# A fused gather layer: tokens ordered by thirty-two on the partitions, weighted sums in eight tiles of 64 by 32, gates on ScalarE

## The reference

```python
def one_block(xb):                      # 128 tokens
    q = jnp.einsum('nd,dc->nc', xb, w_query).reshape(PEER_BLOCK, PEER_HEADS, 2, PEER_QUERY_DIM // 2)
    s = jnp.einsum('nhpc,hpkc->nhpk', q, subkeys).astype(jnp.float32)
    sv, si = lax.top_k(s, PEER_TOPK)
    ...
    top_s, pos = lax.top_k(cand_s, PEER_TOPK)
    experts = jnp.take_along_axis(cand_i, pos, axis=-1).reshape(PEER_BLOCK, PEER_HEADS * PEER_TOPK)
    gates = jax.nn.softmax(top_s, axis=-1).reshape(PEER_BLOCK, PEER_HEADS * PEER_TOPK)
    u = u_table[experts]
    hid = jax.nn.gelu(jnp.einsum('nkd,nd->nk', u, xb).astype(jnp.float32), approximate=False) * gates
    return jnp.einsum('nk,nkd->nd', hid.astype(xb.dtype), v_table[experts])
```

## Time and profile before

| | us |
|---|---|
| median of three runs | 1961.75 (1961.67 to 1966.66) |
| the profiled execution | 1955.42 |
| its span, first to last instruction | 1953.6 |
| PE, DVE, ACT, POOL busy | 1634.3, 1328.8, 656.3, 600.0 |

### The profile page before, as it was taken

One profiled execution on the slowest core, in us unless ns is written; L12 is line 12 of the kernel. 1 busy time (PEld: TensorE's weight loads), 2 busy tenths in 40 slices (PEclk: granted clock), 3 DMA queues, 4 the chain that ended last, 5 costly groups with the idle time before them and its releaser, 6 DMA issues.

```text
span 1953.6 us, 19684 instructions
## 1 busy us (share of the span) xinstructions
PE 1634.3 (84%) x6534; PEld 799.7 (41%) x6534; DVE 1328.8 (68%) x3466; ACT 656.3 (34%) x1224; POOL 600.0 (31%) x529
## 2 busy tenths in 40 slices
PE   7987897779889976888589999789986877877998
PEld 7555553235455443244145434333333322322453
DVE  4356877875788797875876577976665569744242
ACT  3222424242343254222231233521221246311472
POOL 1002333432333343334433333343323325422000
PEclk9997998889999998889899999899998988899999
DMA  7559999999999998999999999999999999999863
GB/s 223 179 169 416 417 417 419 408 417 418 386 413 354 355 416 326 380 419 415 422 413 418 418 414 374 362 400 418 419 417 350 418 419 401 421 418 412 326 235 109
DMA packets 128836, 729.03 MB, mean 373 GB/s; under 512 B 14688, under 2 KB 15856, under 8 KB 63200
## 3 DMA queue, kind: packets, MB, share of 16 engines
q0 software_dynamic: 74272, 537.82, 67.5%
q1 hardware_dynamic: 54464, 189.97, 25.5%
HBM read 725.63 MB, written 2.10 MB: 373 GB/s over the span
## 4 chain that ended last, share of the span: by engine, by line
PE 47%; DMA 23%; DVE 18%; ACT 5%; issue 5%; POOL 1%; POOLq 0%; DVEq 0%; SPq 0%; ACTq 0%
PE pa L919 26%; DMA uv_rows<-in_peer_uv,small 14%; PE py L919 13%; DMA wbuf<-in_wt 8%; PE pb L919 7%; DVE uv_rows L2046 6%; ACT area L1371 2%; ACT L1365 2%; POOL uv_rows L2291 1%; DVE tk L2056 1%; DVE area L2144 1%; DVE tk L2055 1%; DVE small L2033 1%; ACT small L1371 1%; DVE small L1951 0%
## 5 line engine op out<-in xcount | busy, mean ns | idle before, releaser
L2291 POOL DMA_INDIRECT uv_rows<-in_peer_uv,small x512 | 592.2, 1157 | 1182.3 <-PE py L919 967.2
L2046 DVE CUSTOM_DVE_ANT_0 uv_rows<-uv_rows,xrep 128x1024 f32<-128x1024 f32 x512 | 615.7, 1223 | 223.5 <-DMA uv_rows<-in_peer_uv,small 220.6
L919 PE MATMUL py<-uv_rows,tk 128*64 128x512 f32 x2048 | 560.8, 674 | 211.8 <-DVE tk L2056 208.1
L919 PE MATMUL pa<-wbuf,area 128*128 128x512 f32 (+2 forms) x784 | 342.0, 587 | 27.4 <-DMA wbuf<-in_wt 26.7
L1371 ACT ACTIVATE small<-small 128x2 f32<-128x2 f32 (+4 forms) x327 | 70.6, 217 | 849.9 <-DVE small L2046 816.2
L919 PEld LDWEIGHTS py<-uv_rows,tk 128*64 128x64 f32 x2048 | 135.7, 148 | 514.6 <-DVE tk L2056 278.3
L1365 ACT ACT_TABLE_LOAD x250 | 320.8, 1283 | 5.4 <-DVE small L2177 1.0
L919 PE MATMUL pa<-area,wbuf 128*128 128x256 f32 (+2 forms) x1280 | 233.7, 341 | 17.5 <-issue 12.0
L919 PEld LDWEIGHTS pa<-area,wbuf 128*128 128x128 f32 x1280 | 201.3, 199 | 70.6 <-issue 44.5
L919 PEld LDWEIGHTS pa<-wbuf,area 128*128 128x128 f32 (+1 forms) x784 | 134.2, 189 | 229.5 <-issue 176.5
L1371 ACT ACTIVATE area<-pa 128x512 f32<-128x512 f32 (+7 forms) x225 | 89.2, 413 | 267.3 <-PE pa L919 238.0
(11 more groups left out here) (253 smaller groups left out, 1178.0 us busy)
## 6 DMA issues: line engine op xcount, KB each, us to landing
wbuf<-in_wt SPq DMA_DIRECT2D x300, 512.0 KB
uv_rows<-in_wt SPq DMA_DIRECT2D x36, 512.0 KB, 6.6
uv_rows<-in_peer_uv,small POOLq DMA_INDIRECT x512
wbuf<-in_skT SPq DMA_DIRECT2D x11, 256.0 KB
h<-in_x SPq DMA_DIRECT2D x4, 512.0 KB
an<-in_x SPq DMA_DIRECT2D x3, 512.0 KB
out<-h SPq DMA_DIRECT2D x3, 512.0 KB, 8.3
area<-in_finw SPq DMA_DIRECT2D x2, 512.0 KB, 10.1
```

The costliest lines, as they stand in the source:

```text
L919: return nc.tensor.matmul(o, l, r, start=start, stop=stop, skip_group_check=True)
L2046: last = V.tensor_tensor_reduce(uv_rows[:, n % RING, 0:D], uv_rows[:, n % RING, 0:D], xrep[:, b % 2, n % TG, :], 1.0, 0.0, ALU.mult, ALU.a ...
L2291: nc.gpsimd.indirect_dma_start(uv_rows[:, n % RING, :], None, t["peer_uv"], bass.IndirectOffsetOnAxis(ap=expert_ids[:, c:c + 1].bitcast(U3 ...
```

## The change

The tokens are ordered by 32 instead of 64. Quarter q is partitions 32q to 32q+31; of each half of the partitions the pair of gathers serves the half's own 64 tokens, with gather m holding 32 of them with two slots, one in each quarter. So a gather's half of 64 partitions sums to 32 tokens of the same half. `psum_y` is indexed by the half r of the tokens now, and the halves c of the model width stand on its partitions: `psum_y[r][side(c)]`. Each tick has eight products, stationary 64 by 32, moving 64 by 512, on eight places of the array (two halves of its rows, four quarters of its columns), where it had four of 128 by 64. The mask and `mix_w` have 32 columns. Sums are read by four instructions of 64 partitions instead of two of 128, and `xrep` is written twice on all 128 partitions instead of twice on 64. The gates leave VectorE: ScalarE normalizes them in one instruction and spreads them by four, in the plan's place of part 5 of `top_part`, behind a wait for VectorE's reciprocal.

```diff
+def side(r):
+    return slice(TOK * r, TOK * (r + 1))
+def quarter(q):
+    return slice(Q * q, Q * (q + 1))
...
@@ weighted_rows
+                    for r in range(2):
+                        for c in range(2):
+                            mm(psum_y[r][side(c), :], ident[:, side(r)], h1[:, b, W * c:W * (c + 1)], True, False)
+                pe.wait_ge(mix_ready, k + 1)
+                for m in range(TG):
+                    n = BATCH * k + m
                     for c in range(2):
-                        mm(psum_y[c][:, :], ident, h1[:, b, W * c:W * (c + 1)], True, False)
-                pe.wait_ge(mix_ready, k + 1)
-                for lo in range(0, BATCH, TG):
-                    for c in range(2):
-                        for i in range(lo, lo + TG):
-                            n = BATCH * k + i
-                            r = slice(TOK * (n % TG), TOK * (n % TG + 1))
-                            last = mm(psum_y[c][r, :], mix_w[k % 2][:, i, :],
-                                      uv_rows[:, n % RING, D + W * c:D + W * (c + 1)], False, final)
+                        for r in range(2):
+                            last = mm(psum_y[r][quarter(2 * c + m), :], mix_w[k % 2][side(r), m, :],
+                                      uv_rows[side(r), n % RING, D + W * c:D + W * (c + 1)], False, final)
@@ last_scales (ACT)
-                for c in (1, 0):
-                    if c == 0:
-                        act.wait_ge(u_ready, 1)
-                    last = fn(yT_last[:, W * c:W * (c + 1)], psum_y[c][:, :], ACT.Square, accum_out=last_ss[:, 2 * c:2 * c + 1])
-                    if c == 1:
-                        last.then_inc(y1_read, 1)
                 for c in range(2):
                     act.wait_ge(u_ready, c + 1)
...
+                for r in range(2):
+                    for c in range(2):
+                        last = fn(yT_last[side(r), W * c:W * (c + 1)], psum_y[r][side(c), :], ACT.Square,
+                                  accum_out=last_ss[side(r), 2 * c:2 * c + 1])
@@ repeat_rows (ACT)
-                fn(xrep[TOK:P, b % 2, 0, :], xrep[0:TOK, b % 2, 0, :], ACT.Copy)
-                fn(xrep[0:TOK, b % 2, 1, :], xrep[TOK:P, b % 2, 1, :], ACT.Copy).then_inc(xr_ready, 1)
+                for r in range(2):
+                    for m in range(TG):
+                        last = fn(xrep[quarter(2 * r + 1 - m), b % 2, m, :], xrep[quarter(2 * r + m), b % 2, m, :], ACT.Copy)
+                last.then_inc(xr_ready, 1)
+            def gates(g):
+                act.wait_ge(gsum_done, g + 1)
+                at = TOP * (g % (2 * HP))
+                step(fn(gate[:, at:at + TOP], gexps[:, g % 2, :], ACT.Copy, scale=gsum[:, g % 2, 1:2]))
+                for r in range(2):
+                    for m in range(TG):
+                        tok, to = quarter(2 * r + m), quarter(2 * r + 1 - m)
+                        last = fn(gate[to, at + m:at + TOP:TG], gexps[tok, g % 2, 1 - m::TG], ACT.Copy, scale=gsum[tok, g % 2, 1:2])
+                last.then_inc(gate_ready, 1)
@@ the plan on ACT
+                elif name == "tk" and s[3] == 5:
+                    gates(HP * s[1] + s[2])
@@ top_part (DVE), parts 3 and 5
+                    if g >= 2:
+                        dve.wait_ge(gate_ready, g - 1)
...
-                    step(V.reciprocal(gsum[:, g % 2, 1:2], gsum[:, g % 2, 0:1]))
+                    V.reciprocal(gsum[:, g % 2, 1:2], gsum[:, g % 2, 0:1]).then_inc(gsum_done, 1)
                     at = TOP * (g % (2 * HP))
-                    for m in range(TG):
-                        tok = slice(TOK * m, TOK * (m + 1))
-                        for s_ in range(TG):
-                            to = slice(TOK * s_, TOK * (s_ + 1))
+                    step(V.scalar_tensor_tensor(expert_ids[:, at:at + TOP], e01[:, 0, :], float(NK), e01[:, 1, :],
+                                                ALU.mult, ALU.add))
+                    for r in range(2):
+                        for m in range(TG):
+                            tok, to = quarter(2 * r + m), quarter(2 * r + 1 - m)
                             cols = slice(at + m, at + TOP, TG)
-                            V.tensor_scalar(gate[to, cols], gexps[tok, g % 2, s_::TG], gsum[tok, g % 2, 1:2], None, ALU.mult)
-                            last = V.scalar_tensor_tensor(expert_ids[to, cols], e01[tok, 0, s_::TG], float(NK),
-                                                          e01[tok, 1, s_::TG], ALU.mult, ALU.add)
+                            last = V.scalar_tensor_tensor(expert_ids[to, cols], e01[tok, 0, 1 - m::TG], float(NK),
+                                                          e01[tok, 1, 1 - m::TG], ALU.mult, ALU.add)
@@ mix_weights (DVE)
+                dve.wait_ge(gate_ready, k // PER_HEAD + 1)
...
-                V.tensor_tensor(mix_w[k % 2], token_mask.unsqueeze(1).broadcast_to([P, BATCH, TOK]),
-                                wcol[:, k % 2, :].unsqueeze(2).broadcast_to([P, BATCH, TOK]), ALU.mult).then_inc(mix_ready, 1)
+                V.tensor_tensor(mix_w[k % 2], token_mask.unsqueeze(1).broadcast_to([P, BATCH, Q]),
+                                wcol[:, k % 2, :].unsqueeze(2).broadcast_to([P, BATCH, Q]), ALU.mult).then_inc(mix_ready, 1)
@@ take_sums (DVE); last_rows_up has the same loops
-                for c in range(2):
-                    last = V.tensor_copy(h1[:, b, W * c:W * (c + 1)], psum_y[c][:, :])
+                for r in range(2):
+                    for c in range(2):
+                        last = V.tensor_copy(h1[side(r), b, W * c:W * (c + 1)], psum_y[r][side(c), :])
```

More of the change, by code:

```diff
@@ L31 @@
 TOK = P // TG
+Q = P // 4
 BATCH = 2
@@ L546, in build @@
         fw = sb("fw", D)[:, :]
-        tk = Arena(sb("tk", 992 + 2 * BATCH * TOK), 0, 992 + 2 * BATCH * TOK)
+        tk = Arena(sb("tk", 992 + 2 * BATCH * Q), 0, 992 + 2 * BATCH * Q)
         small = Arena(sb("small", 1193), 0, 1193)
@@ L579, in build @@
         iota = small.take(TOP)
-        token_mask = small.take(TOK)
+        token_mask = small.take(Q)
         dots = small.take(8 * BATCH)
@@ L605, in build @@
         wcol = cut(tk.take(2 * BATCH), 2, BATCH)
-        mix_w = [cut(tk.take(BATCH * TOK), BATCH, TOK) for _ in range(2)]
+        mix_w = [cut(tk.take(BATCH * Q), BATCH, Q) for _ in range(2)]
         p1 = Arena(area, 0, AREA)
@@ L711, in build @@
         idx_ready, gmax, gexp = sem("idx_ready"), sem("gmax"), sem("gexp")
+        gsum_done, gate_ready = sem("gsum_done"), sem("gate_ready")
         uv_free = sem("uv_free")
@@ L722, in build @@
         u_ready, sq_done, ss_ready, scales = sem("u_ready"), sem("sq_done"), sem("ss_ready"), sem("scales")
-        half_ready, hw_ready, y1_read = sem("half_ready"), sem("hw_ready"), sem("y1_read")
+        half_ready, hw_ready = sem("half_ready"), sem("hw_ready")
         block = ctx.enter_context(nc.Block())
@@ L1388, in last_scales @@
                 act.wait_ge(uv_free, gather_y(b))
-                for c in (1, 0):
-                    if c == 0:
-                        act.wait_ge(u_ready, 1)
-                    last = fn(yT_last[:, W * c:W * (c + 1)], psum_y[c][:, :], ACT.Square, accum_out=last_ss[:, 2 * c:2 * c + 1])
-                    if c == 1:
-                        last.then_inc(y1_read, 1)
                 for c in range(2):
                     act.wait_ge(u_ready, c + 1)
-                    last = fn(merged_last[:, W * c:W * (c + 1)], an[:, W * c:W * (c + 1)], ACT.Square,
-                              accum_out=last_ss[:, 2 * c + 1:2 * c + 2])
+                    fn(merged_last[:, W * c:W * (c + 1)], an[:, W * c:W * (c + 1)], ACT.Square,
+                       accum_out=last_ss[:, 2 * c + 1:2 * c + 2])
+                for r in range(2):
+                    for c in range(2):
+                        last = fn(yT_last[side(r), W * c:W * (c + 1)], psum_y[r][side(c), :], ACT.Square,
+                                  accum_out=last_ss[side(r), 2 * c:2 * c + 1])
                 last.then_inc(sq_done, 1)
@@ L1982, in expert_rows @@
                 for m in range(TG):
-                    tok = slice(TOK * m, TOK * (m + 1))
-                    last = V.scalar_tensor_tensor(xrep[tok, b % 2, m, :], h1[tok, b, :], rs[tok, 5 + b:6 + b], fw[tok, :],
-                                                  ALU.mult, ALU.mult)
+                    last = V.scalar_tensor_tensor(xrep[:, b % 2, m, :], h1[:, b, :], rs[:, 5 + b:6 + b], fw, ALU.mult, ALU.mult)
                 last.then_inc(xn_done, 1)
@@ L2071, in last_rows_up @@
                 for c in range(2):
-                    if c == 1:
-                        dve.wait_ge(y1_read, 1)
-                    V.tensor_tensor(an[:, W * c:W * (c + 1)], psum_y[c][:, :], weights[:, W * c:W * (c + 1)], ALU.mult)\
-                        .then_inc(u_ready, 1)
+                    for r in range(2):
+                        last = V.tensor_tensor(an[side(r), W * c:W * (c + 1)], psum_y[r][side(c), :],
```

(4 more changed lines are left out.)

1 line of the change is left out of this document (removed).

## The result

The changed kernel takes 1942.72 us (1940.98 to 1943.06, four runs); beside it the kernel before takes 1962.25 (1961.67 to 1966.66). The medians are 19.5 us apart. The ratio, which is taken over all the runs, is 0.9894, with the interval 0.9877 to 0.9911: 1.06% faster, about 21 us. The profiled execution took 1940.98 us, 14.4 less than the one of before.

The account below looks back on a forecast made before the run. DMA at about 418 GB/s bounds most of the run; unfed stretches lack 62 us, TensorE bounding 520 to 680 us. 19.5 + 1.2 + 0.4 won, 2.8 + 1.4 + 0.5 lost: 16.4 us off 1955.4, plus 6.3, gives 1945; range 1925 to 1963.

Parts of the forecast that it names:

- tick on TensorE: The eight products of a tick overlap in two steps, 0.48 + 0.60 = 1.08 us, saving 0.86 us, 44%.
- worth of the shorter tick: Sum over the stretches short of data from 520 to 1510 us, nothing in the fed ones: 19.5 us won.
- of it 520 to 680 us: TensorE bounds this stretch, which lacks 19.1 us against 418 GB/s; 75% of that, 14.3 us, won.
- of it 1460 to 1510 us: py's chain share taken as 6%, as in 740 to 800 and 1190 to 1280 us: 1.3 us won.
- ScalarE's hold, on the path: Five gate activations and a wait for the reciprocal, 2.0 us a head; 2.8 us lost in unfed stretches.
- all beside the tick: Everything but TensorE's shorter tick: 1.2 and 0.4 us won, 2.8, 1.4 and 0.5 us lost.
- Strict order: Rival on TensorE's tick: products do not overlap as forecast, a py tick takes about 4 us; chance 0.08.
- VectorE: Smaller mask product and no gate products on VectorE: 1.2 us won on the chain in three unfed stretches.
- The reading of the sums: At block ends four instructions instead of two, 1.4 us more each: 1.4 us lost at 586 us, 0.5 at the end.
- The opening: First gather 0.4 us earlier; `repeat_rows` 2.1 us longer a block, costing nothing, at most 2.1 each.
- fed-anyway rival: VectorE takes TensorE's place as bound, or the tick keeps four steps: about 1959 us; chance 0.16.
- the rival *ScalarE's hold: Half of ScalarE's 64 us at heads' sixth ticks lies on the path, 32 us lost: about 1974 us; chance 0.08.

Follow-up runs that it names:

- after_again: The changed kernel itself, unaltered, run again on another chip: 1942.12 us, ratio 0.9928 to the kernel before.
- sums_twice: The changed kernel with all eight products of a tick issued twice: 1966.98 us, ratio 1.0038 to the kernel before.
- twice_late: The changed kernel with all eight products of a tick issued twice and ScalarE's gates one tick later: ratio 1.0008 to the kernel before.
- gates_late: The changed kernel with ScalarE's gate activations one tick later, behind the GELU of a head's seventh tick: 1931.61 us, ratio 0.9855.
- before_gates_late: The kernel before with only its gates moved to ScalarE, made one tick later: ratio 0.9984 to the kernel before.
- gates_dve: The changed kernel with its gates back on VectorE: 1939.03 us, ratio 0.9894 to the kernel before.
- late_split: The changed kernel with gates one tick later, the first block's token-row copies later, and finished sums read by VectorE and ScalarE: 1931.33 us, ratio 0.9875.

## Why the prediction came out right

Forecast 1945, measured 1942.72; forecast ratio 1945 to 1961.75, 0.9915, measured 0.9894. By after_again's 0.9928 the gain is even less than the 16.75 us forecast. The mechanism was the one forecast: a TensorE tick of 1.08 us, which pays where data is short and TensorE leads the chain, and nearly nothing where data is the bound. But two terms were too small, with opposite signs, and so partly paid for each other. That the total came out within a few us is to that extent luck.

| step | forecast | shown |
|---|---|---|
| tick on TensorE | 1.08 us | 1.09 us |
| worth of the shorter tick | 19.5 won | 22 to 30 won (sums_twice, twice_late against single products) |
| of it 520 to 680 us | 14.3 won | 10.4 and 14.5 won, heads 6 to 10 |
| of it 1460 to 1510 us | 1.3 won | 4.8 and 4.6 won, heads 22 to 26 |
| ScalarE's hold, on the path | 2.8 lost | 6 to 12 lost (four pairs with late gates, one of them on one chip) |
| all beside the tick | 3.1 lost | about 7 lost (sums_twice), 1.6 with late gates (twice_late) |
| median above the profiled run | 6.3 | 1.7 |

*The tick.* Both kinds of pairs of the earlier trace rows held for eight at once: sixteen instructions took 1.09 us, where the two of one product of 512 columns over the whole array took 1.12 us in the kernel before (at 57.53 us, granted clock 1.00). The 1.08 us is made of 0.48 us, from the first starts in the tick before to the next ones, and the 0.60 us of its last step; that a tick can need no less was my estimate, and no run shows it as a bound. What the runs show is eight starts within 0.047 us, the other eight from 0.454 us on, and 1.09 us in all. Strict order, with its chance of 0.08 and a tick of about 4 us, is refuted by the same 1.09 us.

*What it is worth.* The two numbers of a stretch in the table are the gain between the starts of the heads named, in the two pairs of profiled executions that differ in the doubled products alone (sums_twice and the change, twice_late and gates_late). By them the step from 520 to 680 us was sized right to a few us: TensorE was the bound and data was next. By the rate it gave less than forecast: 393 GB/s where I had expected nearly 410, so 9.5 of the 19.1 us came back. The term that was too small in both pairs is the stretch from 1460 to 1510 us, where I took "the same share as in those two, 6%". Its own chain, and that of the 90 us in which heads 25 and 26 lie:

```profile
by line: issue 25.5%; PE pa L919 19.7%; PE pb L919 17.6%; DVE uv_rows L2046 9.4%; PE py L919 7.5%; ACT area L1371 4.2%; ACT L1365 4.1%; DVE h L2276 2.9%; ACT small L1371 2.9%; DVE area L1800 2.6%; DVE h L1977 1.4%; DVE small L2033 0.9%; DVE
```

```profile
by line: PE pb L919 33.8%; issue 19.1%; PE py L919 14.6%; PE pa L919 10.9%; DVE uv_rows L2046 6.6%; ACT area L1371 2.3%; ACT L1365 2.3%; DVE h L2276 1.6%; ACT small L1371 1.6%; DVE area L1800 1.5%; DVE small L2033 1.3%; DVE area L2163 0.8%;
```
```profile
by line: DMA wbuf<-in_wt 43.1%; PE pb L929 23.4%; PE pa L929 10.8%; DVE uv_rows L2068 10.4%; PE py L929 4.6%; issue 3.8%; ACT area L1381 2.3%; ACT L1375 2.0%; DVE h L2300 1.7%; ACT small L1381 1.6%; DVE h L1999 1.6%; DVE h L2266 1.4%; SPq L
```

The first two are of the kernel before (1460 to 1510, 1420 to 1510 us), the third is of the change (1420 to 1510 us). The 6% was not the slip: py has 7.5% of the stretch, which by my reckoning is 50 x 0.075 x 0.44 = 1.7 us. The slip was the reckoning by py alone. PE together has 45% there (59% over the 90 us), more than any other engine, so it belonged to the first kind, as 520 to 680 us, where I took PE's share of what the stretch lacked: 0.45 x 7.8 = 3.5 us. The bytes show that 4.8 of its 7.8 us came back. The DMA of the weights is late next. That accounts for three to four of the 2 to 10 us that are missing in the sum. The rest can't be placed: between heads 12 and 20, where I had counted nothing, the two pairs show 6.9 and 0.1 us, between 20 and 22 they show 0.6 and 3.8, and behind head 26 they show 5.0 and 1.6. Single executions don't say more.

*VectorE.* The mask product is 225 ns (I took 228), the first gather starts at 143.11 us instead of 143.67 (I took 0.4 earlier). The relief by the gates, net of their activations on ScalarE, is 3 us in the kernel before (before_gates_late) and 7.4 us in the changed one (gates_late against gates_dve); I had 1.2 us for all of VectorE's. That VectorE is the later engine once TensorE's tick is short, as the chains of 520 to 680 and 740 to 800 us show, would explain the difference.

*ScalarE's hold.* Its length was about right, its parts were not: the groups by line and form give

```profile
L1381 ACT ACTIVATE small<-tk 32x8 f32<-32x8 f32 x128 | 38.3, 299 | 2.2
```

299 ns for the small forms, not the 0.22 us of the earlier trace rows, together 1.57 us a head, and 17.8 us of waits in 28 heads, 0.64 us each instead of 0.9. So 2.2 us a head, where I had 2.0. The share on the path was the error: I took a fifth, in seven unfed heads only. The late gates show that it also counted where I had expected nothing (680 to 740 and 1510 to 1812 us), and that the wait in that place does it, or the place itself, not the activations as such.

*The reading of the sums.* 64 partitions take 688 ns, as 128 did (684): four instructions instead of two, as forecast. TensorE's wait there grew from 4.49 to 6.86 us; what that costs in the end is too small for late_split to show.

*The opening.* `repeat_rows` was forecast at "nothing, at most 2.1 each". The first one delays the first `dots` by about that (155.55 against 153.47 us in gates_dve), the gates ahead of it by as much again, and it costs nothing at the end, for the reason given.

*The offset.* I set the profiled run plus 6.3 us. That gap was one between executions of the kernel before, and did not carry over. By its own time the forecast was 1939.0, measured 1940.98.

*PE's busy time.* PE's share was forecast near 73% and is 77%; from 520 to 680 us it fell by 10 us, not 20. py alone did what it should, here over the run, before and then after:

```profile
0.00:1939.00 1939.00, 586.04 (x2096) 145.52 (x2096) 6.58 (x10) 1.38 (x4) 0.93 0.94 376
```
```profile
0.00:1939.00 1939.00, 378.94 (x4160) 59.88 (x4160) 12.38 (x18) 2.82 (x8) 0.86 0.94 376
```

207 us less. But the rest of PE's work took 70 us more. The granted clock fell from 0.93 to 0.86 (next section but one): in the records 69 us of that other work stand at the half clock (granted 0.50) before the change and 207 after it. A py tick of the change took 1.96 us there and 1.09 at the full clock (granted 1.00); if the other work too takes about twice as long, half of these 138 us, 69, are the clock's. Against 44% of a py tick at the full clock I saw 35% of its busy time go. The fed-anyway rival is refuted by the tick of 1.09 us and by the rates of the stretches that had been short of data, which did not stay as they were. Of the rival *ScalarE's hold* a part was true: not 32 us on the path, but 6 to 12.

## What to carry to other kernels

Where one engine leads the chain of a stretch that is short of data, size a gain on it by what the stretch lacks, and not by the share of the one line that gets shorter: from 1460 to 1510 us the share of py gave 1.3 to 1.7 us, PE's share of the lack 3.5, and 4.8 came. Before an in-order engine is given work that waits for another engine, look for a place where its input is long there: the same five activations one tick later, an edit of three lines, gave 0.3 to 0.6% here, though whether the wait or the place did it is open. And read an engine's gain in the time of the steps behind it, not in its busy share: py's busy time fell by 207 us, that of the engine by 137.

## What the runs showed of the hardware

- Eight float32 products on eight places of 64 by 32 ran side by side: sixteen instructions of 512 columns in 1.09 us at a granted clock of 1.00, the first eight 7 ns apart on average (0.047 us for seven steps). Thirty-two on the same places took 1.95 us (sums_twice, at 456.37 us).
- With the shorter tick the granted clock was lower. Over the run it was 0.93 before and 0.86 after, and 0.94 with the products doubled; from 1190 to 1280 us it was 0.85 and 0.61, from 740 to 800 us 0.85 and 0.70. In the former stretch, where PE's busy time fell from 70.41 to 65.02 of 90 us, twelve of the sixteen py ticks took 1.96 us, at a granted clock of 0.50 (0.53 in one of them), most of them behind a wait of PE for VectorE, and three took 1.09, at a granted clock of 1.00:

```profile
1207.39 1.96 PE L929 MATMUL py<-uv_rows,tk 64*32 64x512 f32 x16
1211.50 1.09 PE L929 MATMUL py<-uv_rows,tk 64*32 64x512 f32 x16 [1.57 <-DVE tk L2079]
1219.34 1.96 PE L929 MATMUL py<-uv_rows,tk 64*32 64x512 f32 x16 [2.94 <-DVE tk L2079]
```

  So part of the saving went back through the dense products (70 us more of PE's busy time beside py). That it cost little time, since it fell where data or VectorE was the bound, is an argument; no run held the clock.
- A copy on ScalarE takes as long on 32 partitions as on 64: 1054 ns for 32x1024, 1057 for 64x1024. And a small activation with a scale for each partition takes 299 ns for 32x8, more than the 0.22 us of the 128x16 one without it.
- The median of the kernel before differs by 0.26% between the sets of runs (1957.2 to 1962.25 us), and its single executions spread over more than 10 us on one chip.
